# q and k of layers 1 to 3 multiplied with the tokens stationary, then turned by VectorE and moved between partitions by DMAs

## What is computed

```python
def odd_layer(x, ln, w_in, w_out):                      # layer 1
    h = rmsnorm(x, ln)
    cq, ck, cv, cg = split(h @ w_in, 4)                 # 16 heads of 128
    oc = stick_breaking_attention(heads(cq), heads(ck), heads(cv))
    return x + (oc * silu(cg)) @ w_out

for i in range(2):                                      # layers 2 and 3
    shift, scale, gate = split(silu(c) @ mod_w[i] + mod_b[i], 3)
    h = rms_norm(x, norm_w[i]) * (1 + scale) + shift
    y = dilated_mixer(h, a_w_in) @ a_w_out if i == 0 else moba_mixer(h, b_w_in) @ b_w_out
    x = x + gate * y
```

## Time and profile before

| | |
|---|---|
| median of 3 runs | 2510.06 us (2508.9 to 2510.63) |
| span of the profiled execution | 2507.2 us |
| TensorE matmul busy | 2471.7 us, 99% |
| VectorE / ScalarE / GpSimd busy | 68% / 48% / 2% |
| weights and the rest from HBM | 527.67 MB, 211 GB/s |

### The profile page before, as it was taken

One profiled execution on the slowest core, in us unless ns is written; L12 is line 12 of the kernel. 1 busy time (PEld: TensorE's weight loads), 2 busy tenths in 40 slices (PEclk: granted clock), 3 DMA queues, 4 the chain that ended last, 5 costly groups with the idle time before them and its releaser, 6 DMA issues.

```text
span 2507.2 us, 32901 instructions
## 1 busy us (share of the span) xinstructions
PE 2471.7 (99%) x13110; PEld 2120.8 (85%) x13110; DVE 1695.9 (68%) x2142; ACT 1213.5 (48%) x1637; POOL 41.4 (2%) x51
## 2 busy tenths in 40 slices
PE   8999999999999999999999999999999999999998
PEld 7898888888888887888888888888888878888786
DVE  5887865677877776666566666666665566666655
ACT  5557654544445445444444444444454454444543
POOL 1000000000000000000000000000000000000000
PEclk9999999999999999999999999999999999999999
DMA  7545445687777775887587677767745557677653
GB/s 242 162 136 160 142 138 192 202 263 254 237 223 241 273 249 184 259 264 243 165 258 255 197 247 240 231 211 254 249 135 185 193 172 228 222 226 222 204 194 137
DMA packets 336392, 531.92 MB, mean 212 GB/s; under 512 B 16376, under 2 KB 190784, under 8 KB 336112
## 3 DMA queue, kind: packets, MB, share of 16 engines
q1 hardware_dynamic: 335040, 526.06, 65.7%
q0 software_dynamic: 896, 3.20, 0.4%
q10 hardware_dynamic: 304, 0.57, 0.1%
HBM read 527.67 MB, written 2.10 MB: 211 GB/s over the span
## 4 chain that ended last, share of the span: by engine, by line
PE 63%; issue 30%; DVE 4%; ACT 2%; DMA 0%; POOL 0%; POOLq 0%; SPq 0%; DVEq 0%; ACTq 0%
PE proj L977 20%; PE proj L982 10%; PE proj L996 8%; PE proj L998 8%; PE proj L997 8%; DVE w_lo L1670 2%; PE att L1045 1%; ACT w_hi L1272 1%; PE att L1028 1%; PE att L1091 1%; PE att L1175 1%; DVE slot L1794 1%; PE proj L1003 1%; PE proj L1004 1%; PE proj L1005 0%
## 5 line engine op out<-in xcount | busy, mean ns | idle before, releaser
L1670 DVE TENSOR_TENSOR w_lo<-raw,w_hi 128x1024 fp32r<-128x1024 f32 x804 | 980.9, 1223 | 601.5 <-ACT w_hi L1272 598.7
L1272 ACT ACTIVATE w_hi<-raw 128x1024 fp32r<-128x1024 f32 x804 | 848.1, 1057 | 764.3 <-PE proj L982 410.5
L996 PE MATMUL proj<-w_hi,h 128*128 128x512 f32 (+1 forms) x1800 | 718.7, 399 | 4.6 <-DVE h L1806 3.7
L998 PE MATMUL proj<-w_hi,h 128*128 128x512 f32 (+1 forms) x1800 | 700.4, 389 | 0.0
L997 PE MATMUL proj<-w_lo,h 128*128 128x512 f32 (+1 forms) x1800 | 699.3, 388 | 0.0
L977 PE MATMUL proj<-h,w_hi 128*128 128x512 f32 x2688 | 683.5, 396 | 0.0
L977 PEld LDWEIGHTS proj<-h,w_hi 128*128 128x128 f32 x2688 | 484.1, 189 | 89.0 <-issue 1.4
L996 PEld LDWEIGHTS proj<-w_hi,h 128*128 128x128 f32 x1800 | 339.6, 189 | 72.3 <-issue 8.0
L998 PEld LDWEIGHTS proj<-w_hi,h 128*128 128x128 f32 x1800 | 338.8, 188 | 71.8
L997 PEld LDWEIGHTS proj<-w_lo,h 128*128 128x128 f32 x1800 | 339.7, 189 | 65.2 <-issue 1.0
L982 PEld LDWEIGHTS proj<-h,w_lo 128*128 128x128 f32 x2688 | 366.6, 190 | 26.9
(11 more groups left out here) (232 smaller groups left out, 1460.4 us busy)
## 6 DMA issues: line engine op xcount, KB each, us to landing
raw<-in_a_w_in SPq DMA_DIRECT2D x320, 512.0 KB, 4.6
raw<-in_mod_w SPq DMA_DIRECT2D x192, 512.0 KB, 4.2
raw<-in_w_in_odd SPq DMA_DIRECT2D x128, 512.0 KB, 4.5
raw<-in_b_w_in SPq DMA_DIRECT2D x128, 512.0 KB, 4.0
raw<-in_w_in_even SPq DMA_DIRECT2D x100, 512.0 KB, 3.7
raw<-in_w_out_even SPq DMA_DIRECT2D x32, 512.0 KB, 3.7
raw<-in_w_out_odd SPq DMA_DIRECT2D x32, 512.0 KB, 5.3
raw<-in_a_w_out SPq DMA_DIRECT2D x32, 512.0 KB, 4.1
```

Source lines behind the costliest of these rows:

```text
L996: pe.matmul(o, x_hi[:, xs], hi[:, kk, :], start=start, stop=False)
L998: done = pe.matmul(o, x_lo[:, xs], hi[:, kk, :], start=False, stop=stop)
L1272: act.activation(m.w_hi[u.n % SPLIT_N][:, 0:size], m.raw[i][:, 0:size], ACT.Copy).then_inc(s.hi_ready, 1)
L1670: dve.tensor_tensor(m.w_lo[ring][:, 0:size], m.raw[i][:, 0:size], m.w_hi[ring][:, 0:size].bitcast(F32), ALU.subtract).then_inc(s.lo_dve, 1)
```

## The change

The 40 chunks of 512 columns that hold q and k of layers 1 to 3 (8, 24 and 8 of them; 80 wide chunks before, 320 units either way) get a new form, *turn*. It multiplies as a token chunk does. Then:

- In layer 1 ScalarE copies PSUM into the slot with a scale for each token, for q with a second scale that also holds 1/sqrt(128); in layers 2 and 3 ScalarE does nothing.
- VectorE transposes each 32 by 32 block (one instruction of 128x1024) from the slot (layer 1) or from PSUM (layers 2 and 3) into a new buffer `stage`, of which there is one. Before that it waits until the previous turn's moves have landed.
- GpSimd issues 16 DMAs of 32 KB each, which carry the blocks from each group of 32 partitions of `stage` to each group of 32 partitions of the slot. Where the operand will be the moving one, rows of 1 KB are written as they lie; where it will be the stationary one (`plain`: k in layer 1, q in layers 2 and 3, 20 of the 40) rows are written in pieces of 128 bytes, 256 for each DMA.
- The scores wait for `turn_landed`. Their moving operand is read in runs of 32 elements.

The order in layers 1 and 3 becomes q, k, v. In layer 1 the attention begins 7 slots after the last unit of k, which is one slot before the last unit of the group; in layers 2 and 3 it begins 2 slots after the group's last unit, as before. `H_RING` goes from 10 to 9 places; the 4 KB per partition that this frees are those of `stage`.

```diff
-H_RING = PAIRS + 2
+H_RING = PAIRS + 1
...
+QUAD = 4
+MOVES = QUAD * QUAD
+TURN = UNIT // QUAD
...
+        q = plan.chunk(1, 2, w, c0, "turn", "slot", slot=a, scaled=True, after_av=free)
+        k = plan.chunk(1, 2, w, D + c0, "turn", "slot", slot=a + 1, plain=True, after_av=free)
         v = plan.chunk(1, 2, w, 2 * D + c0, "token", "slot", slot=a + 2, after_av=free)
-        q = plan.wide(1, 2, w, c0, slot=a, scale=float(P) ** -0.5, after_av=free)
-        k = plan.wide(1, 2, w, D + c0, slot=a + 1, after_av=free)
-        plan.run(v)
-        plan.run_wide(q)
-        plan.run_wide(k)
-        qkv.append((q[-1], k[-1], v))
+        for c in (q, k, v):
+            plan.run(c)
+        qkv.append((q, k, v))
...
-    done = [stick_items(plan, g, qkv[g][1].last + 2, 5) for g in range(4)]
+    done = [stick_items(plan, g, qkv[g][1].last + 7, 5) for g in range(4)]
...
-            if k % 3 == 2:
-                c = plan.chunk(2, 4, w, k * D + g * CHUNK, "token", "slot", **place)
-                plan.run(c)
-            else:
-                both = plan.wide(2, 4, w, k * D + g * CHUNK, **place)
-                plan.run_wide(both)
-                c = both[-1]
+            c = plan.chunk(2, 4, w, k * D + g * CHUNK, "token" if k % 3 == 2 else "turn", "slot", plain=k % 3 == 0, **place)
+            plan.run(c)
...
+        q = plan.chunk(3, 6, w, c0, "turn", "slot", slot=a, plain=True, after_pv=free)
+        k = plan.chunk(3, 6, w, D + c0, "turn", "slot", slot=a + 1, after_pv=free)
         v = plan.chunk(3, 6, w, 2 * D + c0, "token", "slot", slot=a + 2, after_pv=free)
...
-    done = [soft_items(plan, 3, g, qkv[g][1].last + 2, 2) for g in range(4)]
+    done = [soft_items(plan, 3, g, qkv[g][2].last + 2, 2) for g in range(4)]
...
             plan.at(c.last + 1, "evac", chunk=c)
+            if c.form == "turn":
+                plan.at(c.last + 1, "turn", chunk=c)
...
+            elif b.turn_n and b.layer >= 2:
+                c.psum_sem, c.psum_n = s.stage_full, b.turn_n
...
+        self.stage = sb("stage", [P, UNIT])
...
+    def stationary(self, i, h, tile):
+
+        return self.slots[i][:, :].rearrange("p (t h n) -> p t h n", t=TILES, h=HPC)[:, tile, h, :]
+
+    def moving(self, i, h):
+
+        return self.slots[i][:, :].rearrange("p (a t h j) -> p t h a j", a=QUAD, t=TILES, h=HPC)[:, :, h, :, :]
+
+    def turn_into(self, c, a):
+
+        if c.plain:
+            return self.slots[c.slot][:, :].rearrange("p (b a j) -> p b a j", a=QUAD, j=FOLD)[:, :, a, :]
+        return self.slots[c.slot][:, a * TURN:(a + 1) * TURN].rearrange("p (b j) -> p b j", j=FOLD)
...
-        if c.form == "token":
+        if c.form in ("token", "turn"):
...
-    w.wait_ge(s.evac_feature, plan.ready[it.layer, it.group][0].feature_n)
+    w.wait_ge(s.turn_landed, 16 * MOVES * plan.ready[it.layer, it.group][0].turn_n)
     h = it.head % HPC
...
+        q = m.stationary(plan.slot_of[it.layer, it.group, "q", g], h, it.tile)
+        k = m.moving(plan.slot_of[it.layer, it.group, "k", g], h)[:, tiles, :, :]
...
+        w.wait_ge(s.turn_landed, 16 * MOVES * plan.ready[1, it.group][1].turn_n)
...
+                w.wait_ge(s.query_scale, 1 if c.scaled else 0)
...
+        elif kind == "evac" and it.chunk.turn_n:
+            c = it.chunk
+            src = m.proj[c.n % 2]
+            if c.layer < 2:
+                src = m.slots[c.slot]
+                w.wait_ge(s.evac_done, c.out_n)
+            w.wait_ge(s.unit_done, c.last + 1)
+            w.wait_ge(s.turn_landed, 16 * MOVES * (c.turn_n - 1))
+            blocks = "p (b g j) -> p b g j"
+            dve.transpose(m.stage[:, :].rearrange("p (g b j) -> p b g j", g=QUAD, j=FOLD),
+                          src[:, :].rearrange(blocks, g=QUAD, j=FOLD)).then_inc(s.stage_full, 1)
...
+                pool.tensor_scalar(m.row_rstd[:, 2, :], m.row_rstd[:, 1, :], float(P) ** -0.5, None,
...
+        elif kind == "turn":
+            c = it.chunk
+            w.wait_ge(s.stage_full, c.turn_n)
+            w.wait_ge(s.av_done, c.after_av)
+            w.wait_ge(s.pv_done, c.after_pv)
+            for a in range(QUAD):
+                for g in range(QUAD):
+                    src = m.stage[a * FOLD:(a + 1) * FOLD, g * TURN:(g + 1) * TURN].rearrange("p (b j) -> p b j", j=FOLD)
+                    pool.dma_start(m.turn_into(c, a)[g * FOLD:(g + 1) * FOLD, :, :], src).then_inc(s.turn_landed, 16)
```

More of the change, by code:

```diff
@@ L181 @@
     wide_n: int = 0
+    turn_n: int = 0
+    scaled: bool = False
+    plain: bool = False
     part: int = 0
@@ L231 @@
     count: int
-ORDER = ["rows", "squares", "split", "mod_start", "mod", "unit", "evac", "resid", "sum", "row", "gate", "mod_fold", "mod_cols",
+ORDER = ["rows", "squares", "split", "mod_start", "mod", "unit", "evac", "turn", "resid", "sum", "row", "gate", "mod_fold", "mod_cols",
          "xn", "hin", "pv", "av", "ho", "ho_copy", "ho_sum", "ho_norm", "ho_scale", "ex", "zp", "wm", "tr", "rc", "hout", "mod_gate", "hg_mm", "hg_cross", "keysT", "queryT", "kT_copy", "qT_copy",
@@ L528, in make_plan @@
         free = 64 + (g - 1) * HPC * TILES if g > 1 else 0
+        q = plan.chunk(3, 6, w, c0, "turn", "slot", slot=a, plain=True, after_pv=free)
+        k = plan.chunk(3, 6, w, D + c0, "turn", "slot", slot=a + 1, after_pv=free)
         v = plan.chunk(3, 6, w, 2 * D + c0, "token", "slot", slot=a + 2, after_pv=free)
-        q = plan.wide(3, 6, w, c0, slot=a, after_pv=free)
-        k = plan.wide(3, 6, w, D + c0, slot=a + 1, after_pv=free)
-        plan.run(v)
-        plan.run_wide(q)
-        plan.run_wide(k)
-        qkv.append((q[-1], k[-1], v))
+        for c in (q, k, v):
+            plan.run(c)
+        qkv.append((q, k, v))
         for key, c in zip("qkv", qkv[-1]):
@@ L598, in number @@
                 c.wide_n = out_n["wide"] = out_n.get("wide", 0) + 1
-        if not c.feature_n or c.func == ACT.Silu:
+        if c.form == "turn":
+            out_n["turn"] = c.turn_n = out_n.get("turn", 0) + 1
+        if c.turn_n and c.layer >= 2:
+            pass
+        elif not c.feature_n or c.func == ACT.Silu:
             out_n[c.to] += 1
@@ L851, in __init__ @@
         self.evac_feature = sem("evac_feature")
+        self.stage_full = sem("stage_full")
+        self.turn_landed = sem("turn_landed")
+        self.query_scale = sem("query_scale")
         self.wide_half = sem("wide_half")
@@ L1018, in tensor_qk @@
         return
[L1019 removed]
+    w.wait_ge(s.turn_landed, 16 * MOVES * plan.ready[it.layer, it.group][0].turn_n)
     h = it.head % HPC
[L1021 to L1022 removed]
+    own = slice(it.tile, it.tile + 1)
+    blocks = [(0, slice(0, it.tile + 1), 0)]
     if it.layer == 2:
[L1024 to L1028 removed]
+        blocks = [(0, slice(0, TILES), 0), (1, own, SEQ), (2, own, SEQ + P)]
+    for g, tiles, at in blocks:
+        q = m.stationary(plan.slot_of[it.layer, it.group, "q", g], h, it.tile)
+        k = m.moving(plan.slot_of[it.layer, it.group, "k", g], h)[:, tiles, :, :]
+        o = m.bank(it.banks[0], at, at + (tiles.stop - tiles.start) * P)
+        done = pe.matmul(o.rearrange("p (t a j) -> p t a j", a=QUAD, j=FOLD), q, k, start=True, stop=True)
     done.then_inc(s.qk_done, 1)
```

26 lines of the change are left out of this document (12 added, 14 removed).

## The result

The changed kernel takes **2496.2 us** (median of 4 runs, 2492.8 to 2497.1) where the kernel before takes 2510.1 (2508.9 to 2510.6): a ratio of 0.9946, 95% interval 0.9934 to 0.9958, 13.8 us less. The prediction said 2492 (2484 to 2545). The profiled execution took 2492.8 us, its span is 2491.0.

A forecast was written before the change was run, and what follows sets the result against it. TensorE's matmul stream was taken to bound the kernel: 2507.2 - 20.6 (matmul form) + 3 (waits at `z`) = 2489.6 us for the span, 2492 with the 2.9 us by which the median lies above it; range 2484 to 2545.

The forecast's parts named there:

- What bounds the kernel: Whole kernel: the time is the sum of TensorE's matmul stream, busy 2471.7 of 2507.2 us; other engines run ahead.
- The form of the matmul, 20.6 us: 320 q and k units: 12 matmuls in place of 16 save 0.069 us in 240 units, 0.05 in 80.
- the rival in which half of it comes: Turned units: only half of the 0.069 us a unit is gained, giving 2500 us; chance 0.08.
- T = 15 us, bounds 12.1 and 30: A plain turn's 16 moves: 15 us from GpSimd's first issue to the last landing, between 12.1 and 30.
- The rival in which an issue takes 1.25 us: Plain turns: GpSimd needs 1.25 us per DMA, not 0.54, so T = 23.4 us and 2526 us; chance 0.20.
- the dear pieces: Plain turns: 128-byte pieces cost as much as 1 KB and crowd the weights; T about 27, 2560 us; chance 0.13.
- `z` waits 0.7 us four times, 3 us: Layer 1, each group's first `z`: TensorE waits T - 14.3 us, 0.7 at T = 15, four times, 3 us more.
- The sign: Whether the change gains or loses: decided at T = 19.5 us, an issue every 1.0 us.
- The ring of 9: `H_RING` of 9: the step delayed by a unit has its first reader 8 units later, so it costs nothing.
- VectorE's wait for `stage` reaches TensorE only from 31 us: VectorE's next transpose waits for the turn before; TensorE feels it only from about 21.8 + 9 = 31 us: nothing.
- DMA load of about 0.9 in plain chunks: Over a plain chunk of 22 us the DMA share rises from 0.77 by 0.2, less 0.07; costs nothing.
- VectorE keeps GpSimd from issuing: Layer 1's input: GpSimd issues only while VectorE is idle, 8.7 us become 36; 2589 us; chance 0.06 with anything else.

The follow-up runs named there:

- start4: The changed kernel with layer 1's attention beginning 4 units behind k's last one instead of 7: 2529.7 us, ratio 1.0081.
- q_late10: start10 with 10 small GpSimd operations ahead of the moves of q's turns in layers 2 and 3: 2519.6 us, ratio 1.0044.
- q_late16: start10 with 16 small GpSimd operations ahead of the moves of q's turns in layers 2 and 3: 2615.3 us, ratio 1.0425.
- q_late24: start10 with 24 small GpSimd operations ahead of the moves of q's turns in layers 2 and 3: 2753.2 us, ratio 1.0971.
- start10: The changed kernel with layer 1's attention beginning 10 units behind k's last one instead of 7: 2492.1 us, ratio 0.9931.
- sixteen: The changed kernel with each turned unit's third product in two matmuls of 256 columns, 16 matmuls a unit: 2513.5 us, ratio 1.0016.
- small_pieces: start10 with all 40 turns plain, moved in pieces of 32 elements (128 bytes): 2491.4 us, ratio 0.9933.
- ring9: The kernel before, with only the ring of `h` shortened (PAIRS + 1 in place of PAIRS + 2): 2512.6 us, ratio 1.0014.
- best: start10 with the layer 0 `hout` transposes that the shorter ring moved sent to PSUM bank 2: 2488.8 us, ratio 0.9919.

## Why the prediction was right, point by point

- **What bounds the kernel**: right. The time followed TensorE's stream in every run. Each wait put into it came out in full and dearer: 27.8 us more of it cost 33.2 (start4), 20.7 cost 27.5 (q_late10), 86.7 cost 123 (q_late16), 224 cost 261 (q_late24), the rest being the clock. The lighter loads of VectorE and ScalarE were worth nothing that the layers' lengths show.
- **The form of the matmul, 20.6 us**: right in size, and in cause for nearly all of it. 3.5 (layer 1, with start10), 12.7 and 3.7 us make 19.9. That rules out the rival in which half of it comes. sixteen put four matmuls a unit back and lost 17.1.
- **The transpose at 1.24 us, read from PSUM too**: right. L1718 takes 1244 ns from PSUM and 1238 from SBUF.
- **Moving operands in runs of 32**: nothing, as said. From one start to the next a score matmul of 256 columns takes 216 ns in layers 2 and 3 (L1028 before, L1057 after) and 215 in layer 1 (L1058 before, L1088 after). It is the same in small_pieces, which reads these operands in runs of 128.
- **T = 15 us, bounds 12.1 and 30**: right, 14.5 to 15.1 us in the four k turns of layer 1, and inside the bounds for all `plain` turns; those with rows of 1 KB take 11.6 to 14.0 where I had 12.1. It is made of other parts, though: GpSimd issues a plain move in 0.58 us (9.25 for 16) and one in rows of 1 KB in 0.49 (7.86), against the 0.54 of the earlier trace rows, and the last one lands about 5 us later where I had 3.4 and the small pieces on top. The pieces themselves cost no more than 8 ns, not 17. And GpSimd's pauses, which no row before the change could show, are in no term. The rival in which an issue takes 1.25 us is out, and so are the dear pieces. The Trainium skill (DMA: Bandwidth & Descriptors, Why small descriptors are slow) has transfers inside SBUF exempt from the loss on small descriptors; small_pieces agrees with that sentence, at 3.4% against 3.3% of the engines. (The rival that the prediction's paragraph on this rule calls the third is the second of its list, the dear pieces.)
- **`z` waits 0.7 us four times, 3 us**: the mechanism is right in group 0 alone, where the turn of 14.5 us met a budget of 14.0 (forecast 14.3) and `z` waited 0.56. In groups 1 and 2 attention of the group before stands between, `z` comes 16.2 us behind the first issue, and nothing waits; in group 3 it waits 1.32 us, for GpSimd's pause. Beginning at 7 units and not at 10 cost 3.9 us by layer 1's length (468.2 to 464.3), of which 1.9 are waits at `z`, 1.1 the two small waits and 0.9 without a row. That this comes near the forecast 3 is partly luck. The sign hung on T even so: by these budgets a turn of 20 us would have made waits of some 20 us in the four groups (an estimate; start4 shows such waits come out in full), as much as the form gained.
- **The ring of 9, "nothing"**: wrong, the term that failed. The prediction has the steps delayed "by a unit"; four of them, one in each layer, move by 14. And I looked only for who reads the delayed step (8 units later) and not for who shares its PSUM bank. It costs 1.9 us of idle, and 3.5 with the clock (ring9; best gives 3.3 back), once, and not at 7 phase changes. It is most of the difference between 2492 and 2496: -19.9 + 3.9 + 1.9 to 3.5 gives -14.1 to -12.5, and the medians differ by 13.8.
- **VectorE's wait for `stage` reaches TensorE only from 31 us**: wrong in size, without effect here. VectorE came to k's transpose 20.4 us after q's (1045.05 to 1065.47 in q_late10), and it has 5 to 6 us in hand, so it is 25.3 to 26.4 us from one transpose to the last landing, and with 1.25 for the transpose a turn of **24 to 25 us**. The step that failed is "splits of 4 more units": of the 8.5 us by which its last `w_lo` is ahead (1073.57 against 1082.03), the transpose, the next `w_lo` and a `mod_w` step need 3.6. The longest turn takes 19.5 us, so nothing of it shows; by this bound the rival with T = 23.4 would still have been priced rightly, and the one with T = 27 too low.
- **DMA load of about 0.9 in plain chunks**: right. Over the 22 us of the first k turn (509.1 to 531.0) the share is 0.91, and 0.97 in the 14.7 us of a plain turn of layer 2 (1046.0 to 1060.7). But its starting point was an average: the same two stretches of the kernel before are at 0.88 and 0.82, not 0.77, so the rise is 0.03 in one and 0.15 in the other where 0.13 was forecast. Over 475 to 846 us the share goes from 0.77 to 0.81, and no weights were late.

```profile
509.10:531.00 21.90, 21.34 (x95) 17.40 (x94) 14.34 (x15) 12.17 (x14) 9.23 (x16) 1.00 0.91 291
1046.00:1060.70 14.70, 14.70 (x67) 12.17 (x66) 9.62 (x9) 5.30 (x5) 9.14 (x16) 1.00 0.97 281
```

- **VectorE keeps GpSimd from issuing**: no. Apart from the pauses, issues stand 0.49 and 0.58 us apart beside a VectorE that is busy three quarters of the time. The Trainium skill (SBUF — State Buffer, SBUF: two separate sides) names two cases of its lock: VectorE in a two-port mode, and, only against a GpSimd operation that reads SBUF, VectorE with two inputs in SBUF. The prediction names the first alone. `w_lo` is of the second kind and fills most of VectorE's time, and the spacing shows that it didn't hold the issues up; so the trace agrees that no lock is at work here.

## What to carry to other kernels

Where TensorE is never idle, count its matmuls as well as its columns: here one matmul more for the same columns cost 17 ns, and 1280 fewer were worth 20 us, more than the work that moved to other engines cost. When a change shortens a ring or moves a step by some units, look at who uses the same buffer or PSUM bank in the new place, not only at who reads the result. And place the first reader of a new chain with some units of room: 7 units of distance gave back all that the form had gained in layer 1, 10 kept it.
